# Joining stages into one block each at three seams of a fused transformer kernel, and picking experts from 70 candidate pairs instead of 256

## What is computed

```python
# end of the first mixer
ys = jnp.stack([y_fox, y_nsa], axis=2)
up = jnp.einsum('bsnc,ncd->bsnd', ys, w_branch)
merged = jnp.sum(g * up, axis=2)
return merged @ w_out                      # first output projection

# experts: 8 heads, 128 keys per half, 16384 experts
s1, i1 = lax.top_k(s[:, :, 0], 16)
s2, i2 = lax.top_k(s[:, :, 1], 16)
cand = (s1[..., :, None] + s2[..., None, :]).reshape(T, 8, 256)
cand_idx = (i1[..., :, None] * 128 + i2[..., None, :]).reshape(T, 8, 256)
top_s, pos = lax.top_k(cand, 16)
idx = jnp.take_along_axis(cand_idx, pos, axis=-1)
w = jax.nn.softmax(top_s, axis=-1)
act = gelu(einsum('cd,chkd->chk', x_c, u[idx_c]))
out = einsum('chk,chkd->cd', w_c * act, v[idx_c])

# second block, attention
o = banded_sink_attention(q, k, v, sinks)
return (o * jax.nn.silu(gate)) @ w_out     # second output projection
```

## Time and profile before

| | |
|---|---|
| median of 3 runs | 1696.38 us (1694.22 to 1697.3) |
| profiled execution, its own time | 1695.42 us |
| its span | 1693.6 us |
| PE busy | 1617.9 us (96%) |
| DVE busy | 1180.8 us (70%) |
| ACT busy | 910.8 us (54%) |
| GpSimd busy | 71.8 us (4%) |
| mean granted clock of TensorE | 0.984 of full |

### The profile page before, as it was taken

One profiled execution on the slowest core, in us unless ns is written; L12 is line 12 of the kernel. 1 busy time (PEld: TensorE's weight loads), 2 busy tenths in 40 slices (PEclk: granted clock), 3 DMA queues, 4 the chain that ended last, 5 costly groups with the idle time before them and its releaser, 6 DMA issues. The chain is left out here.

```text
span 1693.6 us, 33915 instructions
## 1 busy us (share of the span) xinstructions
PE 1617.9 (96%) x12980; PEld 1442.8 (85%) x12980; DVE 1180.8 (70%) x1993; ACT 910.8 (54%) x1618; POOL 71.8 (4%) x38
## 2 busy tenths in 40 slices
PE   7989899999999999998999999999989999999998
PEld 6888788899999999997888888887666989988877
DVE  5556666689989699986666666665764657756565
ACT  4346644454555677765665656653564654435543
POOL 0000000100000000000000000000001333200000
PEclk9979999999999999999999999999999999999999
DMA  6633244555555444435666666642213445310004
GB/s 222 186 101 97 79 153 150 161 185 161 178 171 172 150 125 135 127 125 177 194 191 195 189 194 192 193 144 87 75 51 100 131 145 160 100 52 3 3 28 148
DMA packets 63220, 229.99 MB, mean 136 GB/s; under 512 B 7024, under 2 KB 7280, under 8 KB 63104
## 3 DMA queue, kind: packets, MB, share of 16 engines
q1 hardware_dynamic: 63104, 228.37, 42.9%
HBM read 227.30 MB, written 1.05 MB: 135 GB/s over the span
## 5 line engine op out<-in xcount | busy, mean ns | idle before, releaser
L1089 DVE TENSOR_TENSOR tile_low<-weights,tile_high 128x1024 fp32r<-128x1024 f32 x252 | 307.0, 1221 | 142.3 <-ACT tile_high L1079 138.6
L1079 ACT ACTIVATE tile_high<-weights 128x1024 fp32r<-128x1024 f32 x252 | 268.1, 1064 | 136.5 <-issue 136.5
L178 ACT ACTIVATE tile_high<-weights 128x1024 fp32r<-128x1024 f32 x169 | 178.3, 1057 | 236.2 <-PE banks L230 57.0
L190 DVE TENSOR_TENSOR tile_low<-weights,tile_high 128x1024 fp32r<-128x1024 f32 x146 | 179.5, 1233 | 152.0 <-ACT tile_high L178 129.9
L1141 PE MATMUL banks<-parts,tile_high 128*128 128x256 f32 x2048 | 269.9, 285 | 0.3 <-PEq L1011 0.3
L1443 PE MATMUL banks<-tile_high,parts 128*128 128x512 f32 x1024 | 254.7, 391 | 4.7 <-ACT parts L1408 4.7
L1141 PEld LDWEIGHTS banks<-parts,tile_high 128*128 128x128 f32 x2048 | 254.2, 192 | 0.9 <-issue 0.9
L1443 PEld LDWEIGHTS banks<-tile_high,parts 128*128 128x128 f32 x1024 | 193.2, 189 | 45.0 <-issue 4.9
L230 PE MATMUL banks<-parts,tile_high 128*128 128x272 f32 (+1 forms) x1216 | 171.4, 295 | 4.2 <-PEq L474 3.4
L230 PEld LDWEIGHTS banks<-parts,tile_high 128*128 128x128 f32 x1216 | 159.7, 194 | 13.6 <-issue 10.7
L1146 PE MATMUL banks<-parts,tile_low 128*128 128x256 f32 x1024 | 145.4, 285 | 9.1 <-DVE tile_low L1089 9.1
(11 more groups left out here) (392 smaller groups left out, 2188.4 us busy)
## 6 DMA issues: line engine op xcount, KB each, us to landing
weights<-in_peer_u SPq DMA_DIRECT2D x128, 512.0 KB, 3.5
weights<-in_peer_v SPq DMA_DIRECT2D x128, 512.0 KB, 3.5
weights<-in_dn_in SPq DMA_DIRECT2D x49, 512.0 KB, 3.5
weights<-in_in_t SPq DMA_DIRECT2D x19, 512.0 KB, 3.5
weights<-in_attn_t SPq DMA_DIRECT2D x19, 512.0 KB, 3.6
weights<-in_in_m SPq DMA_DIRECT2D x16, 512.0 KB, 3.6
weights<-in_wq SPq DMA_DIRECT2D x16, 512.0 KB, 3.5
weights<-in_dn_out SPq DMA_DIRECT2D x16, 512.0 KB, 3.6
```

Source lines behind the costliest of these rows:

```text
L178: k.nc.scalar.activation(k.high[:, m % 2, :], k.ring.view(n), ACT.Copy).then_inc(*k.high_made.up())
L190: unit.tensor_tensor(k.low[:, m % 2, :], k.ring.view(n), k.high[:, m % 2, :].bitcast(F32), ALU.subtract).then_inc(*k.low_made[engine].up())
L1079: k.nc.scalar.activation(k.high[:, (s + j) % 2, :], k.ring.buf[:, j % RING, :], ACT.Copy).then_inc(k.high_made.sem, 1)
L1089: k.nc.vector.tensor_tensor(k.low[:, (s + j) % 2, :], k.ring.buf[:, j % RING, :], k.high[:, (s + j) % 2, :].bitcast(F32), ALU.subtract).th ...
```

## The change

Three pairs of stages are each written into one block (`k.joined()`, inside which `k.programs()` gives back the open block instead of a new one), so each engine goes from the first program to the second on its own, held only by the semaphores written down. With it:

- Merge with first output projection: DVE's merge of the last tile (`c` = 7) moves behind the first low part of the projection (`rest_by_vector`). PE waits for the gates of tiles 4 and 5, whose banks it takes. ACT waits for all branch tiles and for the merged pair before each left high part.
- Expert stages: ACT's last Gelu moves behind the first stage copy, DVE's last merge behind the second low part; the out-stage sums in banks 4 to 7 instead of 0 to 3; ACT and PE wait for the last fold; the two row loads of SP move behind four v loads and a wait for the last spreading.
- Sink attention with second output projection: Silu in four pieces of two tiles, the first ahead of the last copies, the other three and the last store behind the projection's first left high part (`rest_by_scalar`). Of the projection's first two weight tiles only one is made early.
- In `out_rows` (all three calls) the first weight's high part stands ahead of the first left part, the second behind it; gates are opened one pair ahead instead of two, each waiting for its piece of Silu and its stored units.
- Candidates: ranks 0, 1 to 4 and 5 to 15 of the first half are paired with the first 16, 8 and 2 of the second, 70 sums in all, in three additions. The position is decoded with the list of where each rank starts (made once by GpSimd): the first index is a sum of differences over the ranks whose start is not above the position, the second rank is position AND width - 1, in some more small operations.
- Pace: `LOOPED` is 72 instead of 80, so 56 tiles are in the second part; low parts come seven in six steps; two low parts stand ahead of `share()`; the 64 groups are spread over one tile fewer at the end.

```diff
+PAIRS = ((0, 1, 16), (1, 4, 8), (5, 11, 2))
+N_PAIR = sum(ranks * partners for _, ranks, partners in PAIRS)
...
-            for c in range(-AHEAD, KC):
+            for c in range(AHEAD):
+                make_low(dve, k, first + c)
+            for c in range(KC - 1):
                 if c + AHEAD < KC:
                     make_low(dve, k, first + c + AHEAD)
...
+                merge(dve, c)
+
+    return lambda dve: merge(dve, KC - 1)
...
-    LOOPED, Q, HOTS, LATE = 10 * BODY, 4, 4, 4
+    Q, HOTS, LATE = 4, 4, 4
     groups, opened = S // Q, LOOPED + 3
-    upto = lambda n: 0 if n < opened else -(-groups * (n - opened + 1) // (NKEY - opened))
+    upto = lambda n: 0 if n < opened else min(groups, -(-groups * (n - opened + 1) // (NKEY - 1 - opened)))
...
-                cand = k.score[:, tt, :, :].rearrange("p a n -> p (a n)").rearrange("p (h a b) -> p h a b", h=PH, a=TOPK)
+                line = k.score[:, tt, :, :].rearrange("p a n -> p (a n)")
+                cand = line[:, 0:PH * N_PAIR].rearrange("p (h s) -> p h s", h=PH)
                 halves = k.top.rearrange("p (h o) a -> p o h a", o=2)
-                nc.vector.tensor_tensor(cand, halves[:, 0].unsqueeze(3).broadcast_to([P, PH, TOPK, TOPK]),
-                                        halves[:, 1].unsqueeze(2).broadcast_to([P, PH, TOPK, TOPK]),
-                                        ALU.add).then_inc(*pick.up())
+                at = 0
+                for rank, ranks, partners in PAIRS:
+                    shape = [P, PH, ranks, partners]
+                    nc.vector.tensor_tensor(
+                        cand[:, :, at:at + ranks * partners].rearrange("p h (a b) -> p h a b", a=ranks),
+                        halves[:, 0, :, rank:rank + ranks].unsqueeze(3).broadcast_to(shape),
+                        halves[:, 1, :, 0:partners].unsqueeze(2).broadcast_to(shape), ALU.add).then_inc(*pick.up())
+                    at += ranks * partners
                 wait()
                 for h in range(PH):
-                    top16(nc, dve, pick, cand[:, h].rearrange("p a b -> p (a b)"), k.best[:, tt, h, :], k.pos[:, h, :])
+                    top16(nc, dve, pick, cand[:, h], k.best[:, tt, h, :], k.pos[:, h, :])
                     yield
...
-                for o, (op, operand) in enumerate(((ALU.logical_shift_right, 4), (ALU.bitwise_and, 15))):
-                    nc.vector.tensor_scalar(flat(k.part), flat(k.pos), operand, None, op).then_inc(*pick.up())
+                keys = k.atf.rearrange("p (h o) a -> p o h a", o=2)
+                eq = line.rearrange("p (h a b) -> p h a b", h=PH, a=TOPK)
+                eq3 = eq.rearrange("p h a b -> p (h a) b")
+                place, width, where, jump = flat(k.partf), flat(k.width), flat(k.part), k.jump
+                nc.vector.tensor_copy(place, flat(k.pos)).then_inc(*pick.up())
+                nc.vector.tensor_copy(jump[:, :, 0:1], keys[:, 0, :, 0:1]).then_inc(*pick.up())
+                nc.vector.tensor_tensor(jump[:, :, 1:TOPK], keys[:, 0, :, 1:TOPK], keys[:, 0, :, 0:TOPK - 1],
+                                        ALU.subtract).then_inc(*pick.up())
+                if tt == 0:
+                    dve.wait_ge(*listed.at(3))
+                for o in range(2):
                     wait()
...
+                    if o == 1:
+                        second = eq[:, 0].rearrange("p a b -> p (a b)")[:, 0:P]
+                        nc.vector.tensor_scalar(width, place, 16.0, 8.0, ALU.is_lt, ALU.mult).then_inc(*pick.up())
+                        nc.vector.tensor_scalar(second, place, 48.0, 6.0, ALU.is_lt, ALU.mult).then_inc(*pick.up())
+                        wait()
+                        nc.vector.tensor_tensor(width, width, second, ALU.add).then_inc(*pick.up())
+                        wait()
+                        nc.vector.tensor_scalar(where, width, 1.0, None, ALU.add).then_inc(*pick.up())
+                        wait()
+                        nc.vector.tensor_tensor(where, flat(k.pos), where, ALU.bitwise_and).then_inc(*pick.up())
+                        wait()
+                        nc.vector.tensor_copy(place, where).then_inc(*pick.up())
+                        wait()
+                    ranks, test = ((starts, ALU.is_ge), (iota[:, 0:TOPK], ALU.is_equal))[o]
...
-                    while n < min(LOOPED, AHEAD + 5 * step // 4):
+                    while n < min(LOOPED, AHEAD + 7 * step // 6):
                         low(n)
                         n += 1
             choose()
-            for m in range(n, LOOPED):
+            for m in range(n, opened - 1):
                 low(m)
             share()
-            for m in range(LOOPED, opened):
-                low(m)
+            low(opened - 1)
             keep_choice()
-            for g in beside(opened):
-                make(g)
             for n in range(opened, NKEY + 1):
                 if n < NKEY:
                     low(n)
+                if n == opened:
+                    for g in beside(n):
+                        make(g)
                 for g in beside(n + 1):
                     make(g)
                 if (n - opened) % 2 == 0:
                     merge(n - 3)
                 for g in beside(n - 1):
                     fold(g)
-            for n in early(k, "v"):
-                make_low(dve, k, n)
-            merge(NKEY - 2)
+            make_low(dve, k, k.tiles["v"])
...
+LOOPED = 9 * BODY
+MERGES = (NKEY - LOOPED) // 2
...
+            for j in range(RING, BODY):
+                fori_load(sp, k, first, src, 0, j)
+            sp.wait_ge(*k.signals["weights_spread"].last())
             sp.dma_start(wide, k.dram["norm_final"]).then_inc(*got.up(16))
             sp.dma_start(k.hm[0:META, :], k.dram["meta"]).then_inc(*got.up(16))
-            for j in range(RING, BODY):
-                fori_load(sp, k, first, src, 0, j)
...
-                    fori_high(act, k, first, i, j)
+                    if type(i) is int and j < AHEAD:
+                        if j == 0:
+                            last_gelu()
+                    else:
+                        fori_high(act, k, first, i, j)
+            act.wait_ge(used.sem, first)
+            act.wait_ge(*k.signals["coef_folded"].last())
             one_round(0)
+            act.wait_ge(*k.signals["gelu_merged"].at(MERGES))
...
-                                ins = nc.tensor.matmul(ps[:, 2 * tt + half, :], c[:, j % STAGES, tt * P:tt * P + P],
+                                ins = nc.tensor.matmul(ps[:, 4 + 2 * tt + half, :], c[:, j % STAGES, tt * P:tt * P + P],
...
-                    fori_low(dve, k, first, i, j)
+                    if type(i) is int and j < AHEAD:
+                        if j:
+                            last_merge()
+                        else:
+                            make_low(dve, k, first + 1)
+                    else:
+                        fori_low(dve, k, first, i, j)
...
-    ahead = dict(zip(range(2, 18, 2), [gate_tile(i) for i in range(AHEAD, fills)] + list(early(k, "attn_out"))))
+    ahead = dict(zip(range(2, 16, 2), [gate_tile(i) for i in range(AHEAD, fills)] + [k.tiles["attn_out"]]))
...
+    def open_gates(q):
+        k.nc.scalar.wait_ge(*gated.at(2 * q + 2))
+        pair = T[:, GATE + 2 * q:GATE + 2 * q + 2, :]
+        nc.scalar.activation(pair, pair, ACT.Silu).then_inc(*opened.up())
...
-            for u in range(len(units) + 2):
+            for u in range(len(units) + 1):
                 if u < len(units):
                     exps(u)
-                if u in ahead:
+                if u == len(units):
+                    open_gates(0)
+                elif u in ahead:
...
-                if u == len(units):
-                    act.wait_ge(*gated.at(fills))
-                    nc.scalar.activation(T[:, GATE:GATE + fills, :], T[:, GATE:GATE + fills, :],
-                                         ACT.Silu).then_inc(*gated.up())
+
+    def last_values(act):
+        store(len(units) - 1)
+        for q in range(1, fills // 2):
+            open_gates(q)
+
...
+    with k.joined():
+        last_values = sink_attention_stage(k)
+        k.split_early.add(k.tiles["attn_out"])
+        opened, stored = k.signals["gate_opened"], k.signals["att_stored"]
+        out_rows(k, "attn_out",
+                 [(k.hm, 0, META, 0)] + [(k.h[:, tt, :], 2 + 2 * tt, P, META + tt * P) for tt in range(NT)],
+                 k.y2, k.tiles["dn_in"] + RING, k.T2[:, 10:18, :], lambda q: opened.at(q + 1), following="dn_in",
+                 scale=[None] + [k.norms[:, 24 + 3 + tt:24 + 4 + tt] for tt in range(NT)],
+                 gate_on=lambda q: stored.at(8 + 2 * q + 2), rest_by_scalar=last_values)
...
+        last_merge = merge_stage(k)
+        merged, gated = k.signals["merged"], k.signals["merge_gated"]
+        out_rows(k, "out1", [(k.h[:, tt, :], 2 * tt, P, tt * P) for tt in range(NT)], k.mergedT,
```

(30 more changed lines are left out.)

166 lines of the change are left out of this document (86 added, 80 removed).

## The result

The changed kernel takes 1673.61 us (median of 4 runs, 1672.73 to 1674.18) against 1696.11 us of the kernel before on the same chip (4 runs, 1694.22 to 1697.3): a ratio of 0.9867, with an interval of 0.9852 to 0.9881. The profiled execution took 1672.73 us with a span of 1671.0. Forecast were 1674.5 us, and 1668.5 to 1682.

A forecast was written before the change was run, and what follows sets the result against it. PE was taken as busy nearly throughout, so only its idle or half-speed time could be won. Gains of 3.9 + 5.9 + 5.7 + 5.9 = 21.4 us gave 1674.5 us, range 1669 to 1681, or 1668.5 to 1682 with two rivals.

The forecast's parts named there:

- (a): Merge to first output projection: PE's idle time falls from 3.18 to 0.9 us and the clock stays up; gain 3.9 us.
- The cover named as thinnest: First output projection: the second low tile is ready at 4.4 us, needed at 4.9, a cover of 0.5 us.
- (b): Expert-in to expert-out: PE's idle time falls from 4.70 to 0.95 us, plus 2.2 of clock; gain 5.9 us.
- (c): Sink attention to second output projection: PE's wait of 4.29 us goes for 0.3, plus 1.7 of clock; gain 5.7 us.
- (d): Picks in expert-in: shorter candidate passes and new pace cut the stage's loss from 12.9 to 7.0 us; gain 5.9, between 2 and 9.5.
- The eight tiles that moved: Expert-in, loop to second part: 12.5 us more DVE work against 23 of PE, DVE's share about 92%, no cost.
- the allowance of 2 us for falls of the clock elsewhere: Outside the changed stretches: clock falls coming earlier or later as everything moves, 2 us within the forecast's bounds.
- Clock falls anyway: Rival: the waits go but the lower clock is granted all the same, at most 5.5 us missing, 1680; chance 0.12.
- the clock's 5.5 us: First tiles after the three seams: half speed costs 1.64, 2.21 and 1.67 us, to be won if the clock stays up.
- Index chain: Rival, in the picks: small operations and their waits give back the savings, 5.9 becomes 0 to 2, 1679 to 1680; chance 0.12.
- Merging without effect: Rival, at the seams: engines still meet between joined programs, so (a) to (c) give nothing, 1690; chance 0.05.
- Slower by a lasting fall: Rival: the clock falls in the picks, at the last index steps, and stays; 60 us at half clock give 1704; chance 0.03.

The follow-up runs named there:

- Order alone: Also written `separate`: the changed kernel with its new order of work, but each stage in a block of its own again; 1680.12 us, ratio 0.9905.
- block alone: Also written `join_only`: the changed kernel with one block per seam, but the pieces around the seams in the old order; 1682.18 us, ratio 0.9916.
- `clock2`: The kernel before, with 4, 6 and 6 unread products on constants filling PE's waits at the three seams; 1696.29 us, ratio 1.0002.
- `share_first`: The changed kernel with the softmax sums ahead of the low parts of tiles 72 and 73 again; 1678.11 us, ratio 0.9886.
- `after_again`: The changed kernel run once more, unchanged; 1673.95 us, ratio 0.9863.
- `paced_whole`: The changed kernel with one low part per 1.66 us of DVE's picking, places for them around the decoding, 2048-column operations whole; 1665.78 us, ratio 0.9827.
- `clock`: The kernel before, with 8, 12 and 12 unread products on constants at PE's three seam waits, twice the filling time planned; 1704.11 us, ratio 1.005.
- `old_picks`: The changed kernel with the old picking: 256 candidates, five low parts in four steps, 80 looped tiles; 1678.01 us, ratio 0.9884.

## Why the prediction was right, point by point

**(a) 3.9 forecast, 3.9 measured.** Idle time 0.81 for 0.9, the first tile 1.5 us shorter for 1.6. The cover named as thinnest held: the second low tile is ready at 235.93 (234.71 + 1.22), its products come at 236.64. Thinner was that of the first low tile, 0.2 us (233.67 and 233.88).

**(b) 5.9 forecast, 5.95 measured.** Idle time 0.88 for 0.95. Order alone and block alone each come within 1 us of it, so the two reasons given (the late merge, the meeting) overlap; the prediction did not split them.

**(c) 5.7 forecast, 6.0 measured.** The step mis-sized is the 0.3 us by which the last copy was to be later: PE's wait before the last values is 1.17 us, not 1.4 (1.09 in rows 4), so 0.1 and not 0.3, and it lies ahead of the mark. The table load takes 1.28 us and Silu starts at its end, 1238.31, as in rows 4. The Trainium skill, ScalarE: Activation LUTs (section What ACT_TABLE_LOAD costs), adds a drain and has 2.66 us in all. By that this part was to give 4.3; the measurement decides: it has no such time between load and Silu, nor ahead of the load, which starts at 1237.02 behind a copy that ends at 1237.00.

**(d) 5.9 forecast, 5.2 measured.** The estimate of a pass over 70 columns (0.425 - 0.195 = 0.230) is 0.231. The decoding, of which no row was there, takes 0.59 us for its first three operations and 1.57 for the six others (401.37 to 401.96 and 411.97 to 413.54 on DVE), 2.2 for the 2.0 taken. The second token tile loses 3.13 us for 3.1. The first loses 3.9: the step that failed is that a wait of under 2 us would leave the clock up, as the one of 1.30 had the earlier trace rows. That wait came as forecast (1.78 at 417.02), and the clock fell behind it; this is 0.8 us, for which the sum had no term. Tile 73 costs 0.86 for 0.7. Together that is 1.0 us less gain than forecast; 0.3 come back from tile 72 on, of which the sum had nothing either.

**The eight tiles that moved** cost nothing that the trace shows: DVE 94% for the 92% forecast, PE full.

**The rest**, 1.5 us net outside these stretches, lies in the allowance of 2 us for falls of the clock elsewhere, and it is chance: the code from the start to the merge is the same in all thirteen traces and takes from 204.1 us (`clock2`) to 208.4 (`share_first`), and in `after_again` the first and the fifth stretch take 208.00 and 485.96 us, no gain over before. The forecast of the whole is so good (0.9 us) because 0.7 too much in (d) stands against 0.3 and 1.5 too little.

**The rivals.** Clock falls anyway: not at the seams of this kernel, but the mechanism is real. The place that the rival named, the gap before the last values, lost the clock in order alone (1.17 us of waiting) and kept it in after (1.17 us too), so its chance of 0.12 was not too high. Waits of 2.10 us (order alone) and 1.78 (after) lost it as well, one of 1.33 kept it. So the short waits helped to win the clock's 5.5 us, they did not secure them. Index chain: its steps lose 7.0 us, 6.3 without the fall of the clock, as calculated; with the low parts of `paced_whole` the same chain loses nothing, so the placing sets it and not the chain. Merging without effect: refuted, PE passes 0.88 us after its last product while DVE's merge is still to come. Slower by a lasting fall: 31.0 us at half clock in all, against 55.6 before.

**Open.** Why the clock falls at a place in one execution and not in another: the wait of 1.17 us at the third seam (order alone and after), the wait of 2.89 us behind the picks (a fall in `share_first` and `clock2`, none in before and `clock`). No run here tells that. What the 72 looped tiles alone are worth was not run.

## What to carry to other kernels

At a seam between stages, write down which single piece the next product waits for, move all others behind it, and only then join the blocks: here each half alone gave some 8.5 of 16 us, and at the seam with the longest chain joining alone gave 0.1. Where one engine prepares tiles for another between its own work, place them by the time of that work and not by a count of steps: with two more places for them in each token tile this took a loss of 7.1 us in the picks to nothing, with the same work. An idle gap of PE has two prices, itself and the next tile at half clock, and one cut to between 1.2 and 2.1 us could still cost the second.

## What the runs showed of the hardware that was not expected

- The clock falls after shorter waits than I had counted on: 1.17 us (order alone, 1244), 1.78 (after, 417), 1.90 (`clock2`, 234), 2.10 (order alone, 233), though not after 1.17 in after, 1.20 (block alone, second seam), 1.30, 1.33 (order alone, second seam), nor after the 2.89 at tile 80 of before. The wait of 1.78 us stands twice in five profiled executions, once in each token tile: behind the first the clock fell in all five (`after`, `after_again`, `separate`, `join_only`, `share_first`), behind the second in one (`join_only`). The Trainium skill, TensorE: Matmul & The Clock Gate (section HAM oscillation — how this bites in real kernels), tells of such falls at waits for data between bursts of products. Its waits are longer than the work of some 2 us between them; falls after single waits of 1.17 and 1.78 us in dense work, and a fall after one wait and none after a longer one, are not in it.
- One fall came without a wait of PE just before it: at 103.95 us in after the clock falls while PE has been busy for all of the 4.00 us from 100 to 104, for the most part with products of 30 columns.
- A single stretch at half clock lasts from 3.4 to 17.1 us in these traces. How long it is at a place differs between executions of the same code there (at 1285 in after 3.41, at 1287 in `old_picks` 6.83). In all it was 31.0 us in the profiled execution of after and 42.0 in that of the same kernel run again, whose span is 2.3 us longer; with each us at half clock worth up to 0.5, that is more than most single steps argued about here, and a reason to compare marks inside the trace and not medians alone.
- One product of 32-bit constants of 384 columns leaves two records of 0.34 us each: 12 records in 4.04 us for 6 calls.
